# The mix of two branches: loops written out, the result kept on chip, the output weights loaded into the normed rows' place

## The chip, the cores and the metric

One NeuronCore of one Trainium2 chip runs the whole program: a first block (attention with compressed keys beside an RWKV branch, a gated mix, a mixture of experts) and two further layers (windowed attention and a recurrent layer, each with experts). The metric is the device time of one execution in microseconds. TensorE does the matrix products, VectorE and ScalarE the elementwise work, SyncE issues most of the DMA transfers. Everything is in float32, and each float32 product of 128 x 128 by 128 x 512 shows as two matmul records.

## The reference, cut to what matters

```python
gates = sigmoid(z_gate + gate_b)                  # (T, 2, D); z_gate = h @ w_in[:, gate columns]
# o_rwkv: y = y_f + y_b, normed over each head of 64:
mu = mean(y); var = mean(square(y - mu))
y = (y - mu) * rsqrt(var + LNX_EPS) * lnx_g + lnx_b
o_rwkv = (y + bonus) * g
mixed = gates[:, 0] * (o_mla @ w_br_mla) + gates[:, 1] * (o_rwkv @ w_br_rwkv)
x = x + mixed @ w_out
h2 = rms_norm(x, norm_ffn_g)                      # then router logits, top 2 of 32 experts
```

T = 1024 tokens, D = 1024 channels; `o_mla` and `o_rwkv` have 512 channels each.

## The kernel before, in words

Each stage is a `Phase`: it owns its on-chip tensors and semaphores and ends with a clearing of the semaphores and a barrier of all engines (line 83 is the barrier). Within a phase each engine has its own program, and semaphores order them. There is no planner; the order on each engine is the order of the code.

**`mix_phase`** holds data transposed: 128 channels on the partitions, 1024 tokens along the row. `h_h_all` (the normed input, `hT` in the code) is on chip already. It has two loops.

The gate loop (4 turns, `j`) computes four gates per turn, gate `2j+u` of branch `b`: 8 products by K and 2 halves of the tokens (`many`, line 1371) into PSUM `pb[2+b]`, and a sigmoid on ScalarE (line 1411) into `sg`, which has room for all 16 gates. Beside them runs the head norm of row block `j` of the RWKV branch: VectorE adds the two directions (`y`, line 1433), TensorE sums over heads with the `ones` matrix (`two`, line 1365), VectorE subtracts the mean (1435), ScalarE squares (1418), TensorE sums again, VectorE makes the variance (1437), ScalarE takes the root (1421), and VectorE inverts it, scales, adds the bonus and multiplies by `g` into `oT` (1439 to 1443); `o_ready` then counts. The sum over `y` stands between gates `(0,0)` and `(0,1)`, the sum over the squares between `(0,1)` and `(1,0)`.

SyncE loads per turn the weights of both branches' gates for `u` = 0 and 1 (line 1336, two places of `wg`, each reused when `z_psum` says that its products are done), then, once `o_ready` says that the one place of `inp` is free, the two y rows (1340), bonus and g (1341, 1342). VectorE waits for all four. `vecs` and `head_ones` are the first two loads of the phase (1329, 1330), and all engines wait for both.

The branch loop (4 turns of 2 blocks) computes `oT` by `w_br_mla` and by `w_br_rwkv`, 16 products per block into two PSUM tensors (line 1371 again). VectorE multiplies both by their gates (1454), adds them (1456) into one of two places `mixed`, and SyncE stores it to `mixT` in DRAM (1351, 1353). `wb` has two places, loaded at line 1348. In SyncE's order the store of a block, with its wait for `mixed_ready`, stands ahead of the weights of the next turn. The phase ends when SyncE has seen all stores land.

**`route_phase`** is written out. SyncE loads the first 256 tokens of `mixT` (line 1579), then half of `w_out`, one x tile, the other half, another x tile (1581, 1582), seven constants (1588) and the rest of `mixT` (1589). TensorE multiplies token tile by token tile, in halves of the columns (`product`, line 1624), with the turning of h2 (1635) and the router's logits (1643) of the tile before in between. VectorE adds x (1696), norms, and at the end works out the choice of experts and the order of the rows.

**`experts_phase`** loops over blocks of 128 gathered rows, with expert weights in two places for pairs of blocks: `wb[0]` belongs to `Moe`, `wb[1]` (`wb1`) and `w2b[1]` to the phase, as do the turned rows `xT`.

At the top, phase "h" (which owns `h_h_all`) ends behind `mix_phase`; `Moe` opens behind it.

Of the kernel before, what the change touches and what calls it, by code (L numbers as in the profile page):

```python
# [13 lines left out]
P = 128  # L14
# [1275 lines left out]
def mix_phase(nc, vecs, w_in, w_br_mla, w_br_rwkv, head_ones, hT, oT_dram, arr_dram, y_dram, mixT_dram):  # L1290

    with Phase(nc, "mix") as ph:
        vec = ph.sb("vec", [P, VEC_N])
# [12 lines left out]
        names = "in_done y_sum mean_psum cent sq_ready var_psum root o_ready consts o_in rt_ready z_psum gates br_psum mixed_ready mixed_out".split()  # L1307
        (in_done, y_sum, mean_psum, cent, sq_ready, var_psum, root, o_ready, consts, o_in, rt_ready, z_psum, gates, br_psum, mixed_ready,
         mixed_out) = [ph.sem(n) for n in names]
        wg_done = [ph.sem(f"wg_done{u}") for u in range(2)]  # L1310
        wb_done = [ph.sem(f"wb_done{u}") for u in range(2)]
        V, A, E, S = (ph.engine(e, n) for e, n in ((nc.vector, "dve"), (nc.scalar, "act"), (nc.tensor, "pe"), (nc.sync, "sp")))
# [3 lines left out]
        mix_view = mixT_dram.rearrange("(k p) t -> p k t", p=P)  # L1316
        wi = w_in[0].rearrange("(k p) n -> p k n", p=P)
        wa = w_br_mla[0].rearrange("(k p) n -> p k n", p=P)
        wr = w_br_rwkv[0].rearrange("(k p) n -> p k n", p=P)

        with nc.Block() as block:

            @block.sync
            def _(sp):
                S.open(in_done, n=64)
                S.open(mixed_out, n=32)
                for u in range(2):
                    S.open(wg_done[u], wb_done[u], n=32)
                sp.dma_start(vec[:, :], vecs).then_inc(consts, 16)
                sp.dma_start(ones[:, :], head_ones).then_inc(consts, 16)  # L1330
                with sp.Fori(0, RJ) as j:
                    for u in range(2):

                        S.hold(z_psum, last(j, 4, 2 * u + 2))
                        for b in range(2):
                            sp.dma_start(wg[:, u, b, :, :], wi[:, :, ds(j * (2 * P) + (GATE_AT + b * D + u * P), P)]).then_inc(wg_done[u], 16)

                    S.hold(o_ready, last(j))
                    for n in range(2):
                        sp.dma_start(inp[:, n:n + 1, :], y_view[:, n, ds(j, 1), :]).then_inc(in_done, 16)  # L1340
                    sp.dma_start(inp[:, 2:3, :], arr_view[:, ARR["bonus"], ds(j, 1), :]).then_inc(in_done, 16)
                    sp.dma_start(inp[:, 3:4, :], arr_view[:, ARR["g"], ds(j, 1), :]).then_inc(in_done, 16)
                sp.dma_start(oT[:, 0:RJ, :], oT_dram.rearrange("(k p) t -> p k t", p=P)).then_inc(o_in, 16)
                with sp.Fori(0, KD // 2) as i:
                    for u in range(2):
# [11 lines left out]
            def _(pe):  # L1357
# [17 lines left out]
                with pe.Fori(0, RJ) as j:  # L1375

                    def gate(u, b):
                        if b == 0:
                            E.hold(wg_done[u], now(j, 32))
# [2093 lines left out]
```

## Time and profile before

| | us |
|---|---|
| three runs, median (lowest, highest) | 4792.51 (4784.24, 4794.08) |
| the profiled execution | 4792.43 |
| its span, first to last instruction | 4790.5 |
| TensorE busy | 4221.4 (88%) |
| VectorE busy | 1579.2 (33%) |
| ScalarE busy | 1072.3 (22%) |
| mean granted TensorE clock | 0.945 of full |
| mix phase, first product to the routing's first product | 1165.44 to 1574.16 |

A row of the timeline merges the instructions of one line that follow each other: its start in us from the start of the span, its length, the engine, the line, what is written from what, how many; in brackets how long the engine stood idle ahead of it and what ended that. PE is TensorE, DVE is VectorE, ACT is ScalarE, SPq is the issuing of DMAs by SyncE. Ends of matmuls are modelled, so a distance is read from start to start.

### The profile page before, as it was taken

The numbers are of one execution on the slowest core, as the hardware profiler recorded it, in microseconds if no ns is written. First come the engines' busy times: TensorE is split into PE (matmuls) and PEld (weight loads), VectorE is DVE, ScalarE is ACT, GpSimd is POOL, SyncE is SP. The second block draws the span as 40 slices with busy tenths as digits, with TensorE's granted clock in tenths as the row PEclk, the third lists the DMA queues.
The fourth block names the chain that finished last, engine by engine and source line by source line (L and its number), as shares of the span: only waits on it lengthen the run. The fifth ranks groups of instructions, "written<-read, shape, count | busy, mean of one in ns | idle before, by whom it ended". The sixth has DMA issues, their size and how long they took to land. (4 is left out here: it accounts for less than half of the span.)

```text
span 4790.5 us, 62335 instructions
## 1 busy us (share of the span) xinstructions
PE 4221.4 (88%) x23090; PEld 2185.5 (46%) x23091; DVE 1579.2 (33%) x2933; ACT 1072.3 (22%) x1830; POOL 267.3 (6%) x304
## 2 busy tenths in 40 slices
PE   7899996887997879988899599999799995999995
PEld 4555444775443444434454344444344442444442
DVE  3365364442221132213483611011156445011012
ACT  1155122443110001111263100000146331000002
POOL 0000001221000001010000000000000000000000
PEclk8899998999998989999999799999899997999998
DMA  2040244332211469964103388888521143888884
GB/s 92 30 172 10 61 171 119 86 79 61 74 63 52 165 217 371 357 232 163 49 1 128 138 302 314 311 310 311 189 68 40 53 160 146 310 304 315 310 310 165
DMA packets 419890, 815.46 MB, mean 170 GB/s; under 512 B 140784, under 2 KB 281968, under 8 KB 386800
## 3 DMA queue, kind: packets, MB, share of 16 engines
q1 hardware_dynamic: 390912, 711.35, 42.9%
q0 software_dynamic: 16704, 60.82, 4.4%
q10 hardware_dynamic: 12080, 40.54, 2.1%
q8 instruction: 142, 2.33, 0.2%
q14 instruction: 52, 0.43, 0.0%
HBM read 686.80 MB, written 125.83 MB: 170 GB/s over the span
## 5 line engine op out<-in xcount | busy, mean ns | idle before, releaser
L2848 PE MATMUL ec0e_pg<-ec_wg,ec0e_xT 128*128 128x512 f32 x1024 | 444.8, 595 | 2.2 <-DVE ec0e_xT L2901 2.2
L2848 PE MATMUL ec1e_pg<-ec_wg,ec1e_xT 128*128 128x512 f32 x1024 | 444.4, 594 | 2.1 <-DVE ec1e_xT L2901 2.1
L2848 PEld LDWEIGHTS ec0e_pg<-ec_wg,ec0e_xT 128*128 128x128 f32 x1024 | 195.4, 191 | 248.7 <-issue 248.7
L2848 PEld LDWEIGHTS ec1e_pg<-ec_wg,ec1e_xT 128*128 128x128 f32 x1024 | 195.3, 191 | 248.3 <-issue 248.3
L1371 PE MATMUL mix_pb<-h_h_all,mix_wg 128*128 128x512 f32 x512 | 224.0, 598 | 12.1 <-DMA mix_wg<-in_w_in_dram 12.1
L3132 PE MATMUL lrui_pA<-lrui_xT,lrui_w 128*128 128x512 f32 x512 | 223.8, 597 | 2.6 <-ACT lrui_xT L3206 2.6
L2874 PE MATMUL ec1e_py<-lru_wd,ec1e_hidT 128*128 128x512 f32 x512 | 223.4, 594 | 0.0
L2874 PE MATMUL ec0e_py<-gqa_wd,ec0e_hidT 128*128 128x512 f32 x512 | 223.3, 594 | 0.0
L679 PE MATMUL front_pz<-h_h_all,front_w 128*128 128x512 f32 x480 | 211.5, 598 | 9.0 <-DMA front_ones<-in_head_ones_dram 9.0
L2889 ACT ACTIVATE ec1e_sg<-ec1e_pg 128x512 f32<-128x512 f32 x32 | 19.2, 599 | 650.0 <-PE ec1e_pg L2848 650.0
L2889 ACT ACTIVATE ec0e_sg<-ec0e_pg 128x512 f32<-128x512 f32 x32 | 19.2, 599 | 648.5 <-PE ec0e_pg L2848 648.5
L2909 DVE TENSOR_TENSOR ec0e_hid<-ec0e_sg,ec0e_pg 128x512 f32<-128x512 f32 x32 | 22.0, 689 | 426.9 <-ACT ec0e_sg L2889 426.9
L2909 DVE TENSOR_TENSOR ec1e_hid<-ec1e_sg,ec1e_pg 128x512 f32<-128x512 f32 x32 | 22.0, 689 | 426.4 <-ACT ec1e_sg L2889 426.4
L1371 PEld LDWEIGHTS mix_pb<-h_h_all,mix_wg 128*128 128x128 f32 x512 | 98.2, 192 | 135.8 <-issue 135.8
L3132 PEld LDWEIGHTS lrui_pA<-lrui_xT,lrui_w 128*128 128x128 f32 x512 | 97.8, 192 | 125.6 <-issue 125.6
L972 POOL TENSOR_TENSOR wkv_a_l<-wkv_a_raw,wkv_tab 128x512 f32<-128x512 f32 x80 | 106.4, 1363 | 786.1 <-ACT wkv_a_raw L988 786.1
L679 PEld LDWEIGHTS front_pz<-h_h_all,front_w 128*128 128x128 f32 x480 | 91.2, 192 | 127.2 <-issue 127.2
L2874 PEld LDWEIGHTS ec1e_py<-lru_wd,ec1e_hidT 128*128 128x128 f32 x512 | 96.0, 190 | 115.5 <-issue 114.8
L2874 PEld LDWEIGHTS ec0e_py<-gqa_wd,ec0e_hidT 128*128 128x128 f32 x512 | 96.0, 190 | 115.3 <-issue 114.8
L1371 PE MATMUL mix_pb<-mix_oT,mix_wb 128*128 128x512 f32 x256 | 119.1, 629 | 32.9 <-DMA mix_wb<-in_w_br_rwkv_dram 30.9
L459 PE MATMUL mlaa_pS<-mla_kT,mla_qT 96*128 96x512 f32 x256 | 129.7, 631 | 4.6 <-ACT mlaa_probs L522 2.5
L1624 PE MATMUL route_po<-route_wo,route_mT 128*128 128x512 f32 x256 | 114.4, 601 | 20.3 <-DMA route_wo<-in_w_out_dram 20.3
(550 smaller groups left out, 6259.4 us busy)
## 6 DMA issues: line engine op xcount, KB each, us to landing
ec_wg<-in_moe_w_gate_up_dram SPq DMA_DIRECT2D x256, 1024.0 KB, 6.5
gqa_wd<-in_moe_w_down_dram SPq DMA_DIRECT2D x128, 512.0 KB, 4.4
lru_wd<-in_moe_w_down_dram SPq DMA_DIRECT2D x128, 512.0 KB, 4.4
moe_wb<-in_w_dram SPq DMA_DIRECT2D x32, 1024.0 KB, 12.7
exp_wb<-in_w_dram SPq DMA_DIRECT2D x32, 1024.0 KB, 12.6
wkv_inp<-arrays SPq DMA_DIRECT2D x160, 128.0 KB, 3.0
arrays<-front_out SPq DMA_DIRECT2D x36, 512.0 KB, 5.7
yb<-mlaa_zero SPq DMA_DIRECT2D x1, 16384.0 KB, 50.6
```

Of the source, the lines that this page charges most:

```text
L459: m = nc.tensor.matmul(pS[:, u % 2 * 2 + j, :], q_all[:, head, tile * P:(tile + 1) * P], k_all[:, head, j * HALF:(j + 1) * HALF], start=Tr ...
L679: m = nc.tensor.matmul(pz[q % 2][:, half * HALF:(half + 1) * HALF], w[:, q % U, k, :], hT[:, k, half * HALF:(half + 1) * HALF], start=k == ...
L972: nc.gpsimd.tensor_tensor(grid(a_l[:, n, :]), grid(a_raw[:, :]), mask(n + 1), ALU.mult).then_inc(a_masked, 1)
L1371: m = nc.tensor.matmul(ps[:, half * HALF:(half + 1) * HALF], weights[:, k, :], rhs[:, k, half * HALF:(half + 1) * HALF], start=k == 0, sto ...
L1624: m = nc.tensor.matmul(po[:, t % 2, halves[h]], mT[:, k, t * P:(t + 1) * P], wo[:, k, halves[h]], start=k == 0, stop=k == KD - 1)
L2848: return nc.tensor.matmul(pg[:, b, :], xT[:, k, :], wg[:, k, b * HALF:(b + 1) * HALF], start=k == 0, stop=k == KD - 1)
L2874: m = nc.tensor.matmul(py[:, b * HALF:(b + 1) * HALF], hidT[:, k, :], wd[:, k, b * HALF:(b + 1) * HALF], start=k == 0, stop=k == KD - 1)
L2889: nc.scalar.activation(sg[:, half * HALF:(half + 1) * HALF], pg[:, half, :], ACT.Silu).then_inc(silu, 1)
L2909: nc.vector.tensor_tensor(hid[:, cols], sg[:, cols], pg[:, 2 + half, :], ALU.mult).then_inc(hid_ready, 1)
L3132: m = nc.tensor.matmul(pA[:, bank, :], w[:, q % W_RING, k, :], xT[:, k, halves[h]], start=k == 0, stop=k == KD - 1)
```

## The change

In `mix_phase` every loop is written out. The weights of a gate have three places (`RING`) and are loaded gate by gate; the two small constants are loaded from ScalarE's queue; the y rows and the bonus and g rows have semaphores of their own. Only gates 0 to 3 (both branches) are computed beside the head norm: two per row block instead of four. Gates 4 to 7 alternate with branch blocks 0 to 3, and `sg` keeps four blocks' gates instead of eight. The branch weights have three places too, and from block 4 on the blocks alternate between two pairs of PSUM tensors. VectorE writes the mixed rows to `mixT`, which is now an on-chip tensor; nothing is stored to DRAM. When the last gate's products are done, SyncE loads the first half of `w_out` into the columns of `hT`, and after the last branch weights the second half. `route_phase` takes both from there and loads neither. `experts_phase` uses `h_h_all` and `mixT` as its second weight buffers and for `xT`. The phase that owns `h_h_all` and a new one that owns `mixT` end behind the experts.

```diff
-def mix_phase(nc, vecs, w_in, w_br_mla, w_br_rwkv, head_ones, hT, oT_dram, arr_dram, y_dram, mixT_dram):
+def mix_phase(nc, vecs, w_in, w_br_mla, w_br_rwkv, head_ones, hT, oT_dram, arr_dram, y_dram, mixT, w_out, wo_in):
...
+        RING, SLOT = 3, 4
...
-        wg = ph.sb("wg", [P, 2, 2, KD, P])
-        wb = ph.sb("wb", [P, 2, 2, RJ, P])
-        sg = ph.sb("sg", [P, 2, KD, T])
-        mixed = ph.sb("mixed", [P, 2, T])
+        wg = ph.sb("wg", [P, RING, KD, P])
+        wb = ph.sb("wb", [P, RING, 2, RJ, P])
+        sg = ph.sb("sg", [P, SLOT, 2, T])
...
+            return (pb[2], pb[3]) if i >= 4 and i % 2 else (pb[0], pb[1])
...
+                def load_g(q):
+                    i, b = q // 2, q % 2
+                    if q >= RING:
+                        sp.wait_ge(z_psum, q - RING + 1)
+                    sp.dma_start(wg[:, q % RING, :, :], wi[:, :, GATE_AT + b * D + i * P:GATE_AT + b * D + (i + 1) * P]).then_inc(wg_in[q % RING], 16)
+                def load_b(i):
+                    if i >= RING:
+                        sp.wait_ge(br_psum, i - RING + 1)
+                    for b, src in enumerate((w_br_mla, w_br_rwkv)):
+                        sp.dma_start(wb[:, i % RING, b, :, :], src[0, :, i * P:(i + 1) * P].rearrange("(k p) n -> p k n", p=P)).then_inc(wb_in[i % RING], 16)
+                def load_y(j):
+                    if j:
+                        sp.wait_ge(o_ready, j)
                     for n in range(2):
-                        sp.dma_start(inp[:, n:n + 1, :], y_view[:, n, ds(j, 1), :]).then_inc(in_done, 16)
-                    sp.dma_start(inp[:, 2:3, :], arr_view[:, ARR["bonus"], ds(j, 1), :]).then_inc(in_done, 16)
-                    sp.dma_start(inp[:, 3:4, :], arr_view[:, ARR["g"], ds(j, 1), :]).then_inc(in_done, 16)
+                        sp.dma_start(inp[:, n:n + 1, :], y_view[:, n, j:j + 1, :]).then_inc(y_in, 16)
+                def load_bonus(j):
+                    sp.dma_start(inp[:, 2:3, :], arr_view[:, ARR["bonus"], j:j + 1, :]).then_inc(bonus_in, 16)
+                    sp.dma_start(inp[:, 3:4, :], arr_view[:, ARR["g"], j:j + 1, :]).then_inc(bonus_in, 16)
+                load_g(0)
+                load_y(0)
+                load_g(1)
+                load_bonus(0)
+                load_g(2)
                 sp.dma_start(oT[:, 0:RJ, :], oT_dram.rearrange("(k p) t -> p k t", p=P)).then_inc(o_in, 16)
-                with sp.Fori(0, KD // 2) as i:
-                    for u in range(2):
-                        S.hold(br_psum, last(i, 2, u + 1))
-                        for b, src in enumerate((wa, wr)):
-                            sp.dma_start(wb[:, u, b, :, :], src[:, :, ds(i * (2 * P) + u * P, P)]).then_inc(wb_done[u], 16)
-                        if u:
-                            S.hold(mixed_ready, now(i, 2, u))
-                            sp.dma_start(mix_view[:, ds(i * 2, 1), :], mixed[:, 0:1, :]).then_inc(mixed_out, 16)
-                    S.hold(mixed_ready, now(i, 2, 2))
-                    sp.dma_start(mix_view[:, ds(i * 2 + 1, 1), :], mixed[:, 1:2, :]).then_inc(mixed_out, 16)
-                sp.wait_ge(mixed_out, 16 * (KD + 2))
+                for i in range(RING):
+                    load_b(i)
+                for j in range(1, RJ):
+                    load_g(2 * j + 1)
+                    load_y(j)
+                    load_bonus(j)
+                    load_g(2 * j + 2)
+                load_g(9)
...
+                load_g(10)
+                for i in range(3, 6):
+                    load_b(i)
+                    load_g(2 * i + 5)
+                    if i < 5:
+                        load_g(2 * i + 6)
+                load_b(6)
+                sp.wait_ge(z_psum, 2 * KD)
+                sp.dma_start(hT[:, :, halves[0]], w_out[0, :, halves[0]].rearrange("(k p) n -> p k n", p=P)).then_inc(wo_in[0], 16)
+                load_b(7)
+                sp.dma_start(hT[:, :, halves[1]], w_out[0, :, halves[1]].rearrange("(k p) n -> p k n", p=P)).then_inc(wo_in[1], 16)
...
+                def gate(i, b, h):
+                    q = 2 * i + b
+                    if h == 0:
+                        pe.wait_ge(wg_in[q % RING], 16 * (q // RING + 1))
+                        if i:
+                            pe.wait_ge(gates, q - 1)
+                    for k in range(KD):
+                        m = nc.tensor.matmul(pb[2 + b][:, halves[h]], wg[:, q % RING, k, :], hT[:, k, halves[h]], start=k == 0, stop=k == KD - 1)
+                    if h == 1:
+                        m.then_inc(z_psum, 1)
...
+                def branches(i):
+                    pe.wait_ge(wb_in[i % RING], 32 * (i // RING + 1))
+                    if i == 0:
+                        pe.wait_ge(o_in, 16)
+                        pe.wait_ge(o_ready, RJ)
+                    elif i == 5:
+                        pe.wait_ge(gates, 2 * KD)
+                        pe.wait_ge(products, 4)
+                    else:
+                        pe.wait_ge(products, i if i < 5 else i - 1)
...
+                for j in range(RJ):
+                    gate(j, 0, 0)
+                    pe.wait_ge(y_sum, j + 1)
+                    if j == 0:
+                        pe.wait_ge(ones_in, 16)
+                    sums(pb[0], y).then_inc(mean_psum, 1)
+                    gate(j, 0, 1)
+                    pe.wait_ge(sq_ready, j + 1)
+                    sums(pb[1], sq).then_inc(var_psum, 1)
+                    gate(j, 1, 0)
+                    gate(j, 1, 1)
+                for i in range(RJ):
+                    branches(i)
+                    for b in range(2):
+                        gate(RJ + i, b, 0)
+                        gate(RJ + i, b, 1)
+                for i in range(RJ, KD):
...
+                    branches(i)
...
+                act.dma_start(ones[:, :], head_ones).then_inc(ones_in, 16)
+                act.dma_start(vec[:, :], vecs).then_inc(v_in, 16)
+                act.wait_ge(v_in, 16)
+                def gate(i, b):
+                    act.wait_ge(z_psum, 2 * i + b + 1)
+                    if i >= SLOT:
+                        act.wait_ge(products, i - SLOT + 1)
...
+                    dve.wait_ge(y_in, 32 * (j + 1))
+                    if j == 0:
+                        dve.wait_ge(v_in, 16)
...
+                def mixed(i):
+                    dve.wait_ge(br_psum, i + 1)
+                    dve.wait_ge(gates, 2 * i + 2)
+                    for b, dst in enumerate((mixT[:, i, :], m1[:, :])):
+                        r = nc.vector.tensor_tensor(dst, banks(i)[b][:, :], sg[:, i % SLOT, b, :], ALU.mult)
+                    r.then_inc(products, 1)
+                    dve.wait_ge(products, i + 1)
+                    V.link(nc.vector.tensor_tensor(mixT[:, i, :], mixT[:, i, :], m1[:, :], ALU.add))
...
-def route_phase(nc, x, w_out, rg_w, rg_b, re_w, re_b, vecs, eye, tables, mixT_dram, x1_dram, h2_dram, slot_u, wts, moe):
+def route_phase(nc, x, wo, wo_in, mT, rg_w, rg_b, re_w, re_b, vecs, eye, tables, x1_dram, h2_dram, slot_u, wts, moe):
...
-        wo = ph.sb("wo", [P, KD, D])
...
-        mT = ph.sb("mT", [P, KD, T])
...
-                sp.dma_start(mT[:, :, 0:EARLY], mix_view[:, :, 0:EARLY]).then_inc(early, 16)
                 for h in range(2):
-                    sp.dma_start(wo[:, :, halves[h]], w_out[0, :, halves[h]].rearrange("(k p) n -> p k n", p=P)).then_inc(wo_in[h], 16)
...
-                sp.dma_start(mT[:, :, EARLY:T], mix_view[:, :, EARLY:T]).then_inc(late, 16)
...
-                pe.wait_ge(early, 16)
...
-                        pe.wait_ge(late, 16)
...
-        wb = [moe.wb[0], ph.sb("wb1", [P, 2, 2, KD, D_EXP])]
-        w2b = [moe.w2b[0], ph.sb("w2b1", [P, 2, 2, D])]
+        wb = [moe.wb[0], spare[0][:, :, :].rearrange("p (u n k) t -> p u n (k t)", u=2, n=2).rearrange("p u n (k f) -> p u n k f", k=KD)]
+        w2b = [moe.w2b[0], spare[1][:, 0:4, :].rearrange("p (u k) d -> p u k d", u=2)]
...
-        xT = ph.sb("xT", [P, R, KD, P])
+        xT = spare[1][:, 4:8, :].rearrange("p s (k t) -> p s k t", k=KD)
...
+        with Phase(nc, "h") as shared:
+            h_all = shared.sb("h_all", [P, KD, T])
+            h_in = shared.sem("h_in")
+            mla_phase(nc, I["x"], I["vecs"], I["w_in"], I["w_uq"], I["w_ukv"], I["eye"], I["mla_rope"], hT, oT, h_all, h_in, yb)
+            front_phase(nc, I["vecs"], I["w_in"], h_all, h_in, I["w_up"], I["a_up"], I["g_up"], I["starts"], I["head_ones"], arrays)
+            wkv_phase(nc, I["wkv_tables"], I["eye"], arrays, yT)
+            with Phase(nc, "mixed") as second:
+                mixT = second.sb("mixT", [P, KD, T])
+                wo_in = [second.sem(f"wo_in{h}") for h in range(2)]
+                mix_phase(nc, I["vecs"], I["w_in"], I["w_br_mla"], I["w_br_rwkv"], I["head_ones"], h_all, oT, arrays, yT, mixT, I["w_out"], wo_in)
+                with Phase(nc, "moe") as third:
+                    moe = Moe(third, I["w1"], I["w3"], I["w2"])
+                    route_phase(nc, I["x"], h_all, wo_in, mixT, I["router_group_w"], I["router_group_b"], I["router_expert_w"],
+                                I["router_expert_b"], I["vecs"], I["eye"], I["route_tables"], x1, h2, slots, weights, moe)
+                    experts_phase(nc, moe, (h_all, mixT), h2, yb)
```

## Rows read from the trace of the kernel before

**Rows 1.** Page, part 1: busy us, share of the span, instructions.

```profile
PE 4221.4 (88%) x23090; PEld 2185.5 (46%) x23091; DVE 1579.2 (33%) x2933; ACT 1072.3 (22%) x1830; POOL 267.3 (6%) x304
```

**Rows 2.** Page, part 5: busy, mean ns, idle before and its releaser.

```profile
L1371 PE MATMUL mix_pb<-h_h_all,mix_wg 128*128 128x512 f32 x512 | 224.0, 598 | 12.1 <-DMA mix_wg<-in_w_in_dram 12.1
...
L1371 PE MATMUL mix_pb<-mix_oT,mix_wb 128*128 128x512 f32 x256 | 119.1, 629 | 32.9 <-DMA mix_wb<-in_w_br_rwkv_dram 30.9
...
L1624 PE MATMUL route_po<-route_wo,route_mT 128*128 128x512 f32 x256 | 114.4, 601 | 20.3 <-DMA route_wo<-in_w_out_dram 20.3
```

**Rows 3.** Timeline, TensorE, gate loop: start us, us, what, idle before.

```profile
1165.44 16.65 PE L1371 MATMUL mix_pb<-h_h_all,mix_wg 128*128 128x512 f32 x32 [12.09 <-DMA mix_wg<-in_w_in_dram]
...
1181.93 1.88 PE L1365 MATMUL mix_pb<-mix_y,mix_ones 128*128 128x512 f32 x4
...
1183.65 13.90 PE L1371 MATMUL mix_pb<-h_h_all,mix_wg 128*128 128x512 f32 x32
...
1197.38 1.88 PE L1365 MATMUL mix_pb<-mix_sq,mix_ones 128*128 128x512 f32 x4
```

**Rows 4.** Timeline, SyncE's queue, start of the mix phase.

```profile
1158.00 0.35 SPq L1329 DMA_DIRECT2D mix_vec<-in_vecs_dram  x1
...
1159.26 3.72 SPq L1336 DMA_DIRECT2D mix_wg<-in_w_in_dram  x4
```

**Rows 5.** DMA issues: KB, us to landing; first line gate weights, last line `w_out`.

```profile
DMA to landing us min/median/max: 4.0/5.1/7.0
...
mix_inp<-yT SPq DMA_DIRECT2D x2, 512.0 KB, 6.0
...
mixT<-mix_mixed SPq DMA_DIRECT2D x2, 512.0 KB, 2.7
...
route_xt<-in_x_dram SPq DMA_DIRECT2D x4, 512.0 KB, 4.0
...
DMA to landing us min/median/max: 11.2/13.6/16.0
```

**Rows 6.** Timeline, TensorE, two groups of branch products.

```profile
1403.84 27.70 PE L1371 MATMUL mix_pb<-mix_oT,mix_wb 128*128 128x512 f32 x64 [2.01 <-issue]
...
1442.05 30.32 PE L1371 MATMUL mix_pb<-mix_oT,mix_wb 128*128 128x512 f32 x64 [10.51 <-DMA mix_wb<-in_w_br_rwkv_dram]
```

**Rows 7.** Windows: us, busy by engine, granted clock, DMA share, GB/s.

```profile
1442.00:1447.00 5.00, 4.95 (x6) 2.19 (x7) 0.00 (x0) 0.00 (x0) 0.00 (x0) 0.50 0.05 15
...
2750.00:2950.00 200.00, 196.41 (x516) 91.16 (x515) 21.05 (x24) 15.79 (x25) 11.16 (x12) 1.00 0.87 307
...
1840.00:1940.00 100.00, 98.98 (x295) 48.18 (x294) 23.33 (x35) 13.87 (x22) 10.38 (x18) 1.00 1.04 363
```

**Rows 8.** Timeline, VectorE, first and last of a normed row's chain.

```profile
1199.41 1.23 DVE L1437 TENSOR_SCALAR mix_rt<-mix_pb 128x1024 f32<-128x1024 f32 x1 [14.22 <-PE mix_pb L1365]
...
1213.94 1.23 DVE L1443 TENSOR_TENSOR mix_oT<-mix_y,mix_inp 128x1024 f32 x1 [0.26 <-DVE mix_y L1442]
```

**Rows 9.** Timeline, all engines, from the mix phase to the routing.

```profile
1556.78 1.22 DVE L1456 TENSOR_TENSOR mix_mixed<-mix_mixed,mix_m 128x1024 f32<-128x1024 f32 x1
1558.39 0.37 SPq L1353 DMA_DIRECT2D mixT<-mix_mixed  x1
...
1574.16 22.26 PE L1624 MATMUL route_po<-route_wo,route_mT 128*128 128x512 f32 x48 [20.32 <-DMA route_wo<-in_w_out_dram]
```

**Rows 10.** Timeline, TensorE, two short stands in later phases.

```profile
2179.24 7.13 PE L2164 MATMUL gqap_pq<-gqa_wd,gqap_xT 128*128 128x512 f32 x16 [3.08 <-DMA gqa_wd<-in_attn_w_qkv_dram]
...
3711.06 10.16 PE L3161 MATMUL lrui_pB<-lru_wd,lrui_gw 128*128 128x512 f32 x16 [3.24 <-ACT lrui_buf L3220]
```

**Rows 11.** Timeline, all engines, change from attention to its tail.

```profile
2539.66 0.42 DVE L2445 TENSOR_TENSOR gqa_oT<-gqaa_ou,gqaa_pO 128x256 f32<-128x256 f32 x1 [2.45 <-ACT gqaa_ou L2397]
...
2540.91 1.52 PE L2566 MATMUL ec0p_po<-gqa_wd,gqa_oT 128*128 128x512 f32 x3 [1.70 <-PEq L83]
```

**Rows 12.** Timeline, TensorE, written-out products of the routing.

```profile
1602.27 10.55 PE L1624 MATMUL route_po<-route_wo,route_mT 128*128 128x512 f32 x24
```

More of the change, by code:

```diff
@@ L1375, in _ @@
[L1375 to L1379, printed above, removed]
-                        E.hold(gates, now(j, 4, 2 * u + b - 1) if u else last(j, 4, 3 + b))
-                        many(pb[2 + b], wg[:, u, b, :, :], KD, hT).then_inc(z_psum, 1)
-                    gate(0, 0)
-                    E.hold(y_sum, now(j))
-                    two(pb[0], ones[:, :], y).then_inc(mean_psum, 1)
-                    gate(0, 1)
-                    E.hold(sq_ready, now(j))
-                    two(pb[1], ones[:, :], sq).then_inc(var_psum, 1)
-                    gate(1, 0)
-                    gate(1, 1)
@@ L1392, in _ @@
-                E.hold(o_ready, RJ + 1)
-                E.hold(gates, 4 * (RJ + 1))
-                pe.wait_ge(o_in, 16)
-                with pe.Fori(0, KD // 2) as i:
-                    for u in range(2):
-                        E.hold(wb_done[u], now(i, 32))
-                        E.hold(mixed_ready, last(i, 2, u + 1))
-                        many(pb[2 * u], wb[:, u, 0, :, :], RJ, oT)
-                        many(pb[2 * u + 1], wb[:, u, 1, :, :], RJ, oT[:, RJ:2 * RJ, :]).then_inc(br_psum, 1)
+                def gate(i, b, h):
[8 more added lines that the diff above has]
+                        m.then_inc(z_psum, 1)
@@ L1442, in _ @@
                     V.link(nc.vector.tensor_tensor(y[:, :], y[:, :], inp[:, 2, :], ALU.add))
-                    V.link(nc.vector.tensor_tensor(oT[:, ds(j + RJ, 1), :].rearrange("p o t -> p (o t)"), y[:, :], inp[:, 3, :], ALU.mult))
+                    V.link(nc.vector.tensor_tensor(oT[:, RJ + j, :], y[:, :], inp[:, 3, :], ALU.mult))
                     dve.sem_inc(o_ready, 1)
-                V.done(RJ)
-                dve.wait_ge(gates, 4 * (RJ + 1))
-                with dve.Fori(0, KD // 2) as i:
-                    V.loop(i, 4)
-                    for u in range(2):
-                        V.hold(br_psum, now(i, 2, u + 1))
-                        V.hold(mixed_out, last(i, 32, 16 * (u + 1)))
-                        for b, dst in enumerate((mixed[:, u, :], m1[:, :])):
-                            r = nc.vector.tensor_tensor(dst, pb[2 * u + b][:, :], sg[:, b, ds(i * 2 + u, 1), :].rearrange("p o t -> p (o t)"), ALU.mult)
-                        V.link(r)
-                        V.link(nc.vector.tensor_tensor(mixed[:, u, :], mixed[:, u, :], m1[:, :], ALU.add))
-                        dve.sem_inc(mixed_ready, 1)
@@ L1461 @@
+                for j in range(RJ):
+                    normed(j)
+                for i in range(KD):
+                    mixed(i)
 N_GROUPS, PER_GROUP = 4, 8
@@ L1563, in route_phase @@
          first_e, in_ready, pos_ready, i_psum, idx_ready) = [ph.sem(n) for n in names]
-        early, late = ph.sem("early"), ph.sem("late")
-        wo_in = [ph.sem(f"wo_in{h}") for h in range(2)]
         x_in = [ph.sem(f"x_in{u}") for u in range(2)]
```

118 lines of the change are left out of this document (38 added, 80 removed).

## The prediction

> **What bounds the kernel now.** I read the granted clock of the one core first, then the page, then its costliest groups, TensorE's waits, the stretches of the mix phase, and last the timelines of each engine in that phase and at its two edges. TensorE is busy 88% of the span [rows 1], so a change counts by the time for which TensorE stands still or runs at half clock. In the stage that is edited, the 512 gate products stand still once (12.1 us) and the 256 branch products 32.9 us (30.9 of them for `mix_wb`), and the routing's products 20.3 us for `route_wo` [rows 2]. Those are what the change can take; the matmuls themselves stay. VectorE's share of the span says nothing here. Its long chain per normed row (part 3) hides behind four gates now, and the change takes away half of that cover.
>
> **Yardsticks.** The product of one gate (32 recorded matmuls) starts at 1183.65 and the next group at 1197.38, so it is 13.73 us; the sum over heads (4 matmuls) is 1.72 us (1181.93 to 1183.65) [rows 3]. All 16 gates, 8 pairs of branch products and 8 sums are computed before and after, in the same instructions: 24 x 13.73 + 8 x 1.72 = 343.3 us of TensorE, unchanged. The sum is made against the profiled execution, 4792.43 us (span 4790.5 us and 1.9 us around it), which is the median of the three runs (4792.51) for all purposes.
>
> **Part 1, the start (+2.9).** TensorE starts at 1165.44 [rows 3]. SyncE's first issue is at 1158.00, but two small loads go first, the weights are issued from 1159.26 on in four issues of 0.93 us each, and TensorE waits for both gates' weights [rows 4]. After, the two small loads go on ScalarE's queue, the gate's weights are the first issue and TensorE waits for those alone. A 512 KB load of gate weights lands 4.0 to 7.0 us after issue (median 5.1) [rows 5]; on an empty queue I take 4.5, so the start is 1162.5, 2.9 us earlier (0.4 to 3.4). The y rows come second (1 MB); their add is wanted after half a gate, 9.6 us after the start with the cold clock, and they have that.
>
> **Part 2, the branch stalls (+39.2).** Now SyncE waits for `mixed_ready` ahead of the next weights, so each second pair of blocks starts late, as at 1442.05 after 10.51 us [rows 6]; there are three of these, 30.9 us [rows 2]. All four groups are busy 119.1 us [rows 2] where 4 x 27.70 = 110.8 would do: 8.3 us. After, weights have three places and are asked for one to three blocks ahead: the nearest case, `load_b(3)`, goes out when the first branch block is done and is wanted after two more blocks and six gates. A load twice its size takes 5.1 us [rows 5]. The wait on `products` ahead of a branch block is covered too: VectorE needs two products and TensorE has two gates (27 us) in between, and from block 5 on the PSUM pairs alternate. 30.9 + 8.3 = 39.2 us go.
>
> **Part 3, what is late next: the y rows (-5.1).** The gate loop now has two gates per normed row, not four, and `load_y(j+1)` still waits for `o_ready`, since there is one `inp`. Count from the start v of the sum of squares (1197.38 [rows 3]). VectorE reads it at 1199.41, and its last product starts at 1213.94 and takes 1.23, so `o_ready` is at v + 17.8 [rows 8]. Then 0.4 us to SyncE's issue (the add ends at 1558.0, the store is issued at 1558.39 [rows 9]), 0.45 for the second issue, the landing, and 1.23 for the add with 0.2 of hand-over. For the landing the nearest row is a 512 KB load right behind another transfer of that size: 4.0 us (`route_xt`); the y rows' own median of 6.0 has two gates' weights ahead of it, which will not be there [rows 5]. y is ready at v + 24.1. TensorE wants it at v + 1.72 + 13.73 + 6.87 = v + 22.3. So it stands 1.7 us, in each of three loops (the first rows are there in time): 5.1 us. Bounds per loop: 0.4 us with the landing of an isolated store (2.7 [rows 5]) and 3.7 us with 6.0, and on top the clock, next.
>
> What a short stand costs in clock, rows show as well: 2.01 us ahead of the branch products cost nothing (27.70 us for 64 is 0.43 each [rows 6]); behind 3.08 us, 16 matmuls took 7.13 us, and behind 3.24 us 10.16 [rows 10], where by the 13.90 for 32 [rows 3] 7.0 would do: 0.1 and 3.1 us. So 1.7 us is taken at nothing. Ends for the three loops together: 1.2 and 3 x (3.7 + 3.1) = 20.4 us.
>
> The Trainium skill speaks against this edit: "TensorE: Matmul & The Clock Gate", section "HAM oscillation — how this bites in real kernels", says that a loop whose products are interrupted by a wait for a DMA each time pays the slow clock again on every turn. By that rule with the price of the worst row, the three loops would cost some 14 us and not 5.1; the trace agrees with it for the wait of 3.24 us and shows no cost at 2.01. It is the first rival below, whose time is worked out without it.
>
> **Part 4, gates to branches (-0.4).** The first branch block now waits for the fourth normed row: `o_ready` at v + 17.8, 0.1 of hand-over, TensorE done at v + 15.5: 2.4 us, where it stood 2.01 before [rows 6]. From here on TensorE has 8 branch blocks and 8 gates, 220 us, with no wait that I can find: a gate's PSUM is free when the sigmoid of two gates earlier is done, and each sigmoid waits for `products` of a block that was finished a gate ago.
>
> **Part 5, the edge to the routing (+13.9).** Now VectorE ends at 1558.0, the store goes out at 1558.39, SyncE waits for it and the barriers and issues the routing's loads, and TensorE starts at 1574.16, when half of `w_out` is there [rows 9]. After, there is no store, the mixed rows are on chip, and `w_out` is asked for when the last gate is done: 55 us of branch products are left, 41 us for its second half, against 11.2 to 16.0 us for such a load now (median 13.6 [rows 5]). What is left is the barrier: in another phase change VectorE ends at 2540.08 and TensorE starts at 2540.91, 0.83 us later [rows 11]. I take 1.0, so the start is 15.2 us earlier (14.4 to 15.4). The routing starts at half clock before and after: it costs 1.5 us now (22.26 for 48 matmuls [rows 9] where 20.8 would do), and I take the 2.8 of the mix phase's own start (16.49 for 13.73 [rows 3]), so -1.3 (+1.5 to -1.3). The x rows and constants are issued at once; they now land behind 4 MB of weights and will then have the queue alone. The first use of the constants is 22 us after TensorE's start.
>
> **Part 6, the rest (-0.5).** Of the barriers at phase ends, one goes from this edge and two are added behind the experts; with the last instructions around it one takes 0.83 us at most [rows 11], and I take 0.5 (0 to 0.8). The experts' second buffers lie in the places of the normed and the mixed rows, but are filled by the same loads at the same points. The written-out products cost nothing: the routing is written out already, and there 24 matmuls take 10.55 us [rows 12], and by the loop's 13.90 for 32 they would take 10.5.
>
> **The sum:** 2.9 + 39.2 - 5.1 - 0.4 + 13.9 - 0.5 = 50.0 us. 4792.4 - 50.0 = 4742.4 us. All of it stays, since everything behind hangs on the routing's result and only starts sooner.
>
> **Rivals.**
> (a) The y rows come late enough for the clock to fall: 6.0 us of landing, so 3 x 3.7 = 11.1 us, and the mean of the two priced stands (0.1 and 3.1) on each, 4.8: 15.9 for 5.1, 4753 us; at worst 20.4, 4758. For it: the 6.0 row, and that the bonus and g rows are issued right behind. Against: `route_xt`'s 4.0.
> (b) The output weights don't do what they are fetched early for: some transfer still holds the routing's start for 10 us. 4752 us. Against: 41 us of cover.
> (c) The gain is swallowed by the experts, whose loads run at 363 GB/s [rows 7]: 4790 us, no change. Against: TensorE is busy 99.0 of 100 us there, and the loads need the routing's choice, so they move with it.
> (d) Slower: straight-line code. The loops' bodies are replaced by 800 matmuls in a row with their weight loads; if these had to be fetched at a pace below TensorE's, each would need to start 62 ns later (0.492 for 0.430 us) to eat the 50 us, and at 0.50 the kernel takes 4799 us. Against it stands the routing's row [rows 12].
> (e) The longer unbroken run (220 us) is granted a lower clock: against it, 200 us of the later experts at clock 1.00 [rows 7]; it counts with (d).
>
> **Chances.** Forecast 78%, (a) 13%, (b) 3%, (c) 3%, (d) and (e) together 3%. A measurement of this kernel can tell 0.2%, 9.6 us, from no change. Faster: 0.94; same 0.03; slower 0.03. Low end: 1.2 for the loops, no loss at the edge's clock, 0.5 at the start, 4736.7, and single runs lie up to 8 us apart around the median: 4733. High end: rival (a) with 4 us more, 4757.
>
> **What will show it.** Right: TensorE starts near 1162.5; three waits of 1 to 3 us for VectorE's y in the gate loop, followed by groups without loss; one of 2.4 us ahead of the first branch block; then no wait and clock 1.00 until the last product, near 1516.6; the routing's first product 5.3 us behind it. Wrong: waits of over 3 us for y with half clock behind them (a); a DMA as releaser of the routing's first product (b); the stretch behind the routing longer than before (c); a mean distance of matmuls above 0.43 us at clock 1.00 (d).

## The result, and the profile after

| us | before | after |
|---|---|---|
| median of the runs (lowest, highest) | 4788.47 (4784.24, 4794.08), 4 runs | 4734.23 (4731.53, 4735.47), 4 runs |
| profiled execution, its span | 4792.43, 4790.5 | 4735.36, 4733.2 |
| mean granted clock | 0.945 | 0.949 |

The ratio is 0.9882, 95% interval 0.9868 to 0.9897: 1.2% faster. The medians are 54.2 us apart, the profiled executions 57.1; the forecast was 50.0. (The prediction's sum starts at the profiled execution of the kernel before, 4792.43 us, which lies 4.0 us above the median of the four runs.) Taken again later, beside new runs of the kernel before, the changed kernel took 4732.67 us (4725.16 to 4733.73, 5 runs), 0.9878 of it (0.9862 to 0.9895).

The page's groups of the changed kernel that answer to [rows 2], with the idle time behind the last bar:

```profile
L1385 PE MATMUL mix_pb<-h_h_all,mix_wg 128*128 128x512 f32 x512 | 224.6, 598 | 8.8 <-DMA mix_wg<-in_w_in_dram 8.8
...
L1646 PE MATMUL route_po<-h_h_all,mixed_mixT 128*128 128x512 f32 x256 | 115.5, 606 | 5.2 <-PEq L83 5.2
```

The branch products are no longer in the list: they don't wait for weights any more. TensorE's timeline through the mix phase into the routing (start, length, what, how many; in brackets a stand ahead and what ended it):

```profile
1162.16 9.73 PE L1385 MATMUL mix_pb<-h_h_all,mix_wg 128*128 128x512 f32 x16 [8.81 <-DMA mix_wg<-in_w_in_dram]
1171.73 1.88 PE L1391 MATMUL mix_pb<-mix_y,mix_ones 128*128 128x512 f32 x4
...
1180.31 1.88 PE L1391 MATMUL mix_pb<-mix_sq,mix_ones 128*128 128x512 f32 x4
1182.03 20.76 PE L1385 MATMUL mix_pb<-h_h_all,mix_wg 128*128 128x512 f32 x48
1202.63 1.88 PE L1391 MATMUL mix_pb<-mix_y,mix_ones 128*128 128x512 f32 x4
...
1274.73 13.90 PE L1385 MATMUL mix_pb<-h_h_all,mix_wg 128*128 128x512 f32 x32
1288.66 11.82 PE L1407 MATMUL mix_pb<-mix_oT,mix_wb 128*128 128x512 f32 x27
...
1453.54 55.10 PE L1407 MATMUL mix_pb<-mix_oT,mix_wb 128*128 128x512 f32 x128
1513.87 23.38 PE L1646 MATMUL route_po<-h_h_all,mixed_mixT 128*128 128x512 f32 x48 [5.24 <-PEq L83]
```

No bracket stands between the first gate and the routing: the y rows are never late, and the first branch block starts 0.2 us behind the last gate (1288.66 against 1274.73 + 13.73). From 1302 to 1450 the clock is full:

```profile
1162.16:1168.00 5.84, 5.84 (x8) 2.51 (x9) 1.23 (x1) 0.00 (x0) 0.00 (x0) 0.55 1.07 397
1302.00:1450.00 148.00, 148.00 (x346) 65.55 (x345) 14.32 (x12) 7.79 (x7) 0.00 (x0) 1.00 0.12 32
```

(Window, its length, busy time by engine, granted clock, DMA share, GB/s.) From 1162.16 to 1168.00 it is 0.55, near the lower of the two levels. The gain of the span, 57.3 us, is this:

| | before | after | gain | forecast |
|---|---|---|---|---|
| end of the stage before (1153.35 in both) to the first gate product | 12.09 | 8.81 | 3.3 | 2.9 |
| first gate product to the last branch product | 388.4 | 346.5 | 41.9 | 33.7 |
| last branch product to the routing's first | 20.3 | 5.2 | 15.1 | 15.2 |
| from there to the end of the span | 3216.3 | 3219.3 | -3.0 | -1.8 |

### The profile page after: what moved, and what is told of

Read it like the earlier page. It is cut to its first block and busy times, and to the rows that moved or that the text cites. A ratio compares the mean times of both kernels' runs of the same rounds, so it can differ in the third digit from the quotient of the medians.

```text
span 4733.2 us, 61819 instructions
## 1 busy us (share of the span) xinstructions
PE 4216.9 (89%) x23090; PEld 2186.2 (46%) x23091; DVE 1578.3 (33%) x2933; ACT 1068.2 (23%) x1827; POOL 267.2 (6%) x304
## 5 line engine op out<-in xcount | busy, mean ns | idle before, releaser
L3180 PE MATMUL lrui_pB<-lru_wd,lrui_gw 128*128 128x512 f32 x256 | 117.8, 619 | 6.5 <-ACT lrui_buf L3239 6.5
L1646 PE MATMUL route_po<-h_h_all,mixed_mixT 128*128 128x512 f32 x256 | 115.5, 606 | 5.2 <-PEq L83 5.2
```

The costliest lines, as they stand in the source:

```text
L1646: m = nc.tensor.matmul(po[:, t % 2, halves[h]], mT[:, k, t * P:(t + 1) * P], wo[:, k, halves[h]], start=k == 0, stop=k == KD - 1)
L3180: m = nc.tensor.matmul(pB[:, at, :], gw[:, u % 2, z, k, c, :], xc[:, u // 2 * 2 + c, halves[h]], start=c == 0, stop=c == 1)
```

## The experiments

**1. Why the normed rows are not late.** The changed kernel's ScalarE and VectorE in the first turn:

```profile
1180.51 1.11 ACT L1440 ACTIVATE mix_sg<-mix_pb,mix_vec 128x1024 f32<-128x1024 f32 x1 [3.19 <-PE mix_pb L1385]
1181.64 1.28 ACT L1449 ACT_TABLE_LOAD   x1
1183.49 1.06 ACT L1449 ACTIVATE mix_rt<-mix_rt 128x1024 f32<-128x1024 f32 x1 [0.56 <-DVE mix_rt L1466]
```
```profile
1182.23 1.22 DVE L1466 TENSOR_SCALAR mix_rt<-mix_pb 128x1024 f32<-128x1024 f32 x1 [7.36 <-PE mix_pb L1391]
1184.58 6.55 DVE L1470 RECIPROCAL mix_rt<-mix_rt 128x1024 f32<-128x1024 f32 x1 [1.12 <-ACT mix_rt L1449]
...
1194.53 1.23 DVE L1474 TENSOR_TENSOR mix_oT<-mix_y,mix_inp 128x1024 f32<-128x1024 f32 x1
1200.83 1.23 DVE L1462 TENSOR_TENSOR mix_y<-mix_inp 128x1024 f32<-128x1024 f32 x1 [5.07 <-DMA mix_inp<-yT]
```

The table of the square root is loaded at 1181.64, before `rt` exists (VectorE is done with it at 1183.45); ScalarE then waits. In the kernel before, the load came behind that wait, since VectorE's `rt` ended the gap ahead of it:

```profile
1200.74 1.28 ACT L1421 ACT_TABLE_LOAD   x1 [1.84 <-DVE mix_rt L1437]
```

From the start v of the sum of squares, v = 1180.31, `o_ready` is at v + 15.45, where it was at v + 17.8 [rows 3, 8]. Theory A: that is the form of the wait. In the loops each wait was an instruction of its own with a semaphore increment behind it (`hold`); written out, it is a plain wait against a constant. Rival B is that the chain got shorter by something else, fewer loads beside it or constant addresses. Two runs put the increment back:

```diff
                     act.wait_ge(rt_ready, j + 1)
+                    act.sem_inc(A.pace, 1)
                     nc.scalar.activation(rt[:, :], rt[:, :], ACT.Sqrt).then_inc(root, 1)
```

> The changed kernel with one semaphore increment between ScalarE's wait for rt_ready and the square root, so that the wait stands alone, as it does in the loops of the kernel before. Theory A (in the written-out program the load of ScalarE's table goes ahead of the wait, and that is most of why the chain of a normed row is shorter than forecast): the table load moves behind rt again, VectorE's reciprocal starts about 3.6 us behind the start of rt and not 2.35, the chain grows by 1.3 us, the y rows come 0.7 us late in each of three turns and the first branch block by 1.3 us; the mix phase takes about 3.4 us longer. Rival B (the chain is shorter because the loads beside it are fewer or the addresses constant): nothing moves.

```profile
1181.27 1.28 ACT L1451 ACT_TABLE_LOAD   x1 [1.94 <-DVE mix_rt L1468]
1182.56 1.06 ACT L1451 ACTIVATE mix_rt<-mix_rt 128x1024 f32<-128x1024 f32 x1
```
```profile
1201.37 1.98 PE L1392 MATMUL mix_pb<-mix_y,mix_ones 128*128 128x512 f32 x4 [0.87 <-DVE mix_y L1464]
...
1290.83 13.97 PE L1408 MATMUL mix_pb<-mix_oT,mix_wb 128*128 128x512 f32 x32 [1.40 <-DVEq L1477]
```

The table load is behind `rt` again, `o_ready` is at v + 16.8 (15.45 in the changed kernel), and TensorE stands 0.87, 0.66 and 0.76 us for y and 1.40 ahead of the branches: 3.7 us where it stood 0.2, as expected (3.4 us more). (The one time taken, 4731.33 us, can't show 3.5 us: single runs of one kernel lie up to 17 us apart, and a good part of that is spent ahead of this stage, whose predecessor ended anywhere between 1149.0 and 1158.1 us in the profiles.) The second run adds, to that increment, `dve.sem_inc(V.pace, 1)` behind the wait ahead of the reciprocal and behind each of VectorE's five chained steps:

> The same increment on ScalarE and one behind the wait ahead of the reciprocal and behind each of the five chained steps of VectorE, as the loops of the kernel before have them. Theory A with its second half (each such stand-alone wait costs VectorE some 0.15 us): the chain from the start of the second sum to o_ready is 17.8 us again as before (15.45 in the changed kernel), TensorE stands 1.7 us for the y rows in three turns and 2.4 us ahead of the first branch block, and the kernel takes some 7 us longer, close to the forecast 4742. Rival B: no more than 1 us longer.

```profile
1201.30 1.98 PE L1392 MATMUL mix_pb<-mix_y,mix_ones 128*128 128x512 f32 x4 [1.42 <-DVE mix_y L1464]
...
1292.68 15.67 PE L1408 MATMUL mix_pb<-mix_oT,mix_wb 128*128 128x512 f32 x32 [2.09 <-DVEq L1483]
```

```profile
1177.40 1.88 PE L1392 MATMUL mix_pb<-mix_sq,mix_ones 128*128 128x512 f32 x4
```
```profile
1193.59 1.22 DVE L1481 TENSOR_TENSOR mix_oT<-mix_y,mix_inp 128x1024 f32<-128x1024 f32 x1
```

`o_ready` is at v + 17.4, and TensorE stands 1.42, 1.35, 1.31 and 2.09 us (1.7, three times, and 2.4 expected), with 1.7 us of half clock behind the last (15.67 for 13.97), which was not expected. From the first gate product to the last branch product it takes 8.5 us more than the changed kernel. The time is 4741.66 us (4738.49 to 4745.15, 4 runs; 0.9905 of before, 0.9888 to 0.9921). That is 0.7 us from the forecast, but in part by luck, since the half clock makes up for stands that were shorter than forecast; and its interval overlaps that of the changed kernel (0.9868 to 0.9897), so the trace shows the difference and the time only suggests it.

Theory A holds for most of the chain: of the 2.35 us, the place of the table load is 1.36 and the increments on VectorE are 0.6. The last 0.4 us didn't come back, and what they were is not shown; rival B may have a share in them. So the forecast priced a chain with the old form of waits.

**2. What a stand costs in clock, rival (a).** Three runs let the y rows come later, by asking ahead of them for loads that stand behind them in the changed kernel (and, in the third, for a row that nothing reads):

```diff
 # 1 MB ahead                  # 1.5 MB ahead                # 2 MB ahead
+sp.wait_ge(o_ready, j)       +sp.wait_ge(o_ready, j)       +sp.wait_ge(o_ready, j)
+load_bonus(j)                +load_bonus(j)                +load_bonus(j)
                              +load_g(2 * j + 2)            +load_g(2 * j + 2)
                                                            +sp.dma_start(extra, y_view[:, 0, 0:1, :]) ...
 load_y(j)                     load_y(j)                     load_y(j)
```

> The changed kernel with the bonus and g rows (1 MB) asked for ahead of the y rows. The y rows should land 2.8 us later (1 MB at some 370 GB/s), so TensorE stands about 2.2 us in each of three turns. Theory C (a stand this short costs no clock): the group of 16 matmuls behind it stays at 7.03 us, the kernel takes 6.6 us longer. Rival D, rival (a) of the forecast (a stand repeated in every turn drops the clock): groups of 8 to 10 us behind each, 10 to 15 us longer in all.

> As the run with the bonus rows first, with the next gate weights (512 KB) ahead of the y rows as well: 1.5 MB, so a stand of about 3.6 us in each of three turns. If the price in clock sets in at about 3 us, as the two rows of the kernel before say (0.1 us behind 3.08, 3.1 behind 3.24), the matmuls behind each cost between 0 and 3 us more; if short stands never cost clock, nothing: 11 us longer in all without the clock, up to 20 with it.

> As the run with the bonus rows first, and the next gate weights and one more load of 512 KB (a y row again, into a place that nothing reads) ahead of the y rows too: 2 MB, so the y rows land some 5.6 us later and TensorE stands about 5 us in each of three turns. Theory C (the price in clock grows with the length of the stand): each costs 1.5 to 3.1 us in the matmuls behind it, 20 to 24 us longer in all. Rival: stands alone, 15 us longer, the groups behind them unchanged.

TensorE in the second turn of each, in this order of the kernels:

```profile
1201.09 3.38 PE L1392 MATMUL mix_pb<-mix_y,mix_ones 128*128 128x512 f32 x4 [2.66 <-DVE mix_y L1463]
1204.31 7.03 PE L1386 MATMUL mix_pb<-h_h_all,mix_wg 128*128 128x512 f32 x16
```
```profile
1201.67 3.78 PE L1392 MATMUL mix_pb<-mix_y,mix_ones 128*128 128x512 f32 x4 [3.26 <-DVE mix_y L1463]
1205.25 8.17 PE L1386 MATMUL mix_pb<-h_h_all,mix_wg 128*128 128x512 f32 x16
```
```profile
1208.82 3.78 PE L1398 MATMUL mix_pb<-mix_y,mix_ones 128*128 128x512 f32 x4 [4.52 <-DVE mix_y L1469]
1212.39 7.45 PE L1392 MATMUL mix_pb<-h_h_all,mix_wg 128*128 128x512 f32 x16
```

The sum of four matmuls takes 1.98 behind a short stand and 3.78 at half clock, the 16 gate matmuls 7.03 at full clock. With the two runs of experiment 1, that makes 17 stands:

| stand, us | how many | lost in the matmuls behind it |
|---|---|---|
| 0.66 to 1.42 | 7 | nothing |
| 2.01, 2.09, 2.58, 2.66 | 4 | 0, 1.7, 0, 1.4 |
| 3.26 to 5.28 | 6 | 1.8 to 3.0 each |

The first gate product to the last four blocks took 300.8, 312.1 and 311.5 us against 291.4 in the changed kernel: 9.4, 20.7 and 20.2 longer, for 6.6, 11 to 20 and 20 to 24 expected; the times were 4740.66, 4750.44 and 4756.71 us, one run each. The stands were 2.4, 4.0 and 4.5 us on average (2.2, 3.6 and 5 expected). So rival (a) had a real price, but its condition, late y rows, didn't come about in the changed kernel. No stand of the forecast's 1.7 us was measured: the nearest are 1.42 (free), 2.01 (free, here and in [rows 6]) and 2.09 (1.7 us lost). From 2.0 to 2.7 us some stands lose the clock; all of 3.26 us and over did. The kernel before has one of 3.08 us that cost 0.1 [rows 10].

**3. The branch stalls alone.** The kernel before, with SyncE's part of the branch loop written out and in another order, and nothing else (the store semaphore is split in two for it). There SyncE asked for the weights only behind the store, 5 us before TensorE's product at 1442.05:

```profile
1436.10 0.37 SPq L1353 DMA_DIRECT2D mixT<-mix_mixed  x1
1437.06 0.41 SPq L1348 DMA_DIRECT2D mix_wb<-in_w_br_mla_dram  x1
```

The new order:

```diff
+                for n in range(KD):
+                    if n + 2 < KD:
+                        sp.wait_ge(br_psum, n + 3)
+                        load_b(n + 2)
+                    sp.wait_ge(mixed_ready, n + 3)
+                    sp.dma_start(mix_view[:, n:n + 1, :], ...)
```

> The kernel before with one part alone: SyncE asks for a branch block's weights as soon as the products of two blocks earlier are done, ahead of the store of mixed rows, in its two places; everything else, the loops too, stays. Theory (the stalls are SyncE's order, not the number of places): the three waits of 10 us and the half clock behind them go, 39 us faster. Rival (two places are too few, or the store and the loads disturb each other): waits of some us stay, under 30 us faster.

```profile
1408.50 110.11 PE L1377 MATMUL mix_pb<-mix_oT,mix_wb 128*128 128x512 f32 x256 [2.01 <-issue]
```

All eight blocks in one run of 110.11 us, in two places of weights. 4753.80 us (4748.08 to 4759.62, 4 runs), 0.9919 of before (0.9903 to 0.9936): 31 to 46 us. In the trace the stage is 388.4 - 348.3 = 40.1 us shorter, 39 expected. Most of the change's gain is this order on one queue; a third place, the unrolled loops of the other engines and the interleaving are not needed for it.

**4. The edge.** Two runs of the changed kernel undo it step by step: first the two loads of `w_out` go back to the start of the routing, then the mixed rows also go to DRAM block by block, the phase waits for the stores, and the routing loads them again.

```diff
-                sp.dma_start(hT[:, :, halves[0]], w_out[0, :, halves[0]]...
+                for h in range(2):          # in the routing
+                    sp.dma_start(wo[:, :, halves[h]], w_out[0, :, halves[h]]...
```

> The changed kernel with the output weights loaded in the routing again, as before, into the same place. Theory: the mixed rows on chip bring little by themselves, since the weights still have to land: TensorE starts the routing some 8 us later than in the changed kernel (its two loads landed in 7.4 us median there), 8 to 10 us longer. Rival (the barrier and the reload of the mixed rows were the wait, the weights came beside them): under 3 us longer.

> As the run before this one, and the mixed rows are stored to DRAM and loaded again in the routing, as before: the edge as the kernel before has it. The last block's store and its landing cost about 3 us ahead of the barrier, and 1 MB of mixed rows ahead of the weights another 3: 14 to 15 us longer than the changed kernel. If it costs less, part of the edge's gain has another source than these two edits.

```profile
1519.96 22.73 PE L1644 MATMUL route_po<-h_h_all,mixed_mixT 128*128 128x512 f32 x48 [12.76 <-DMA h_h_all<-in_w_out_dram]
```
```profile
1526.60 22.57 PE L1655 MATMUL route_po<-h_h_all,mixed_mixT 128*128 128x512 f32 x48 [17.52 <-DMA h_h_all<-in_w_out_dram]
```

Stands of 12.8 and 17.5 us for 5.2: 7.5 us for the weights (8 to 10 expected), 4.8 more for the way through DRAM, 12.3 together (14 to 15 expected). The times are 4740.91 (4739.07 to 4741.65) and 4743.45 us (4739.47 to 4746.52), four runs each (0.9897 and 0.9900 of before); their intervals, 0.9880 to 0.9913 and 0.9883 to 0.9916, overlap each other's and the changed kernel's, so these prices are read in the trace. The kernel before stood 20.3, so 2.8 of the 15.1 us belong to neither: 1.3 lie between the last product and the first load (one phase end more, and the looped tail), 1.5 in a slower landing of the first half (11.7 against 10.2 us from SyncE's first issue to the product). That rest wasn't separated further.

**5. Keeping TensorE busy across the two waits.** Three products that nothing reads while the first weights are on their way, and some behind the last block:

```diff
+                for n in range(3):
+                    nc.tensor.matmul(pb[1][:, 0:HALF], hT[:, 0, 0:P], hT[:, 0, 0:HALF], start=True, stop=True)
...
+                for n in range(5):
+                    nc.tensor.matmul(pb[0][:, 0:HALF], ones[:, :], oT[:, 0, 0:HALF], start=True, stop=True)
```

> The changed kernel with eight products more, whose results nothing reads: three at the start of the mix phase, while the first gate's weights are on their way, and five behind the last branch block, while VectorE finishes the mixed rows. Theory C (half clock is the price of the stand ahead of it, and work of any kind avoids it): the first 16 gate matmuls take some 7.5 us and not 9.7, the routing's first 48 take 20.8 and not 23.4, so some 4.5 us shorter in the trace, a tenth of a per cent. Rival: the clock falls at the phase change anyway (the barrier's 1 us), then the routing's 23 us stay.

> As the run kept warm, and the last branch block computed by halves of the tokens, so that VectorE multiplies and adds the first half while TensorE computes the second. VectorE's tail ahead of the barrier shrinks from 4.5 us to some 2.5: 2 us on top of the run kept warm, 6 to 7 us under the changed kernel. If the tail is not what the barrier waits for, nothing on top.

> As the run by halves, with three products that nothing reads behind the last block and not five. In the run by halves VectorE ended 2.6 us behind the last real product but TensorE's filler only after 4.45, and the routing began 5.3 us behind that product, as without halves. If the filler held the barrier, the routing now begins 3.5 us behind the last product and its first 48 matmuls still take 20.8 us: 1.8 us shorter in the trace from the last product on. Rival: the barrier costs the 5.3 us whatever ends ahead of it, or the clock falls in the gap and the 48 take over 22 us.

> The changed kernel once more, on the chip of the two others, to compare with: 4728 to 4740 us.

The run by halves, and then the one with the shorter filler, from the filler to the routing:

```profile
1507.50 4.45 PE L1439 MATMUL mix_pb<-mix_oT,mix_ones 128*128 128x512 f32 x10
1512.82 20.84 PE L1666 MATMUL route_po<-h_h_all,mixed_mixT 128*128 128x512 f32 x48 [0.86 <-PEq L83]
```
```profile
1507.12 2.74 PE L1439 MATMUL mix_pb<-mix_oT,mix_ones 128*128 128x512 f32 x6
1510.86 20.84 PE L1666 MATMUL route_po<-h_h_all,mixed_mixT 128*128 128x512 f32 x48 [1.00 <-PEq L83]
```

The clock holds over the 1 us of the barrier: 20.84 us for 48 matmuls, for 23.38. In the run kept warm the first 16 gate matmuls take 7.39 for 9.73 (8.86 to 10.14 in the runs without filler). But three products at half clock last 5.5 us, longer than the wait that they fill: the first gate product came 9.6 us behind the stage before and not 8.8, so the start gained 1.6 us. Halves alone brought nothing (5.3 us from the last product to the routing, as before), because the filler had become what the barrier waits for; with the shorter one it is 3.7. From the end of the stage before to the end of the routing's first 48, the changed kernel takes 383.7 us (383.1 the second time), kept warm 379.6, by halves 379.6, with the shorter filler 377.1. The times are 4727.02 (0.9868, 0.9850 to 0.9887), 4732.52 (0.9877, 0.9861 to 0.9894) and 4728.30 us (0.9867, 0.9850 to 0.9883) beside 4732.67 (0.9878) for the changed kernel: the intervals of the ratios overlap, so the 6.6 us are seen in the trace and not in the time.

## Why the prediction was right or wrong

The direction, the places and their order were right, and 4734.23 us lies in the range, but 1.2 us above its low end, and in the profiled executions the gain was 7 us larger than the sum. Those 7 us are the 5.1 of part 3 and the 2.2 of part 4; the smaller errors of the other parts cancel.

- **Part 3 failed (-5.1 forecast, 0 measured)**, and with it **part 4 (-0.4 forecast, +1.8)**. The step was "`o_ready` is at v + 17.8": it took VectorE's chain from the loop of the kernel before. Measured v + 15.45. What follows in that step came out: y was wanted at v + 22.3 (22.32: the sum of squares at 1180.31, the next sum over y at 1202.63), and from the chain's end to the add it took 5.07 us where its terms give 5.05. The second is partly luck: SyncE issued 0.1 us behind `o_ready` and not 0.4, and landing and hand-over took 4.6 us and not 4.2. y was there at v + 21.75, 0.6 us ahead. Experiment 1 gives 2.0 of the 2.35 us back, and the stands come with them. The omission stands in part 6: "the written-out products cost nothing" looked at TensorE alone and never asked what unrolling does to ScalarE and VectorE.
- **Part 2 (39.2)** was right in its mechanism and 0.9 us short (40.1 in experiment 3): 27.70 for an undisturbed group holds 0.2 us of modelled end, which was counted into each of four groups, and 0.2 us of the 40.1 are a shorter half clock at that run's first gate.
- **Part 1** 3.3 for 2.9: SyncE's first issue was at 1157.64, 0.4 us earlier, and the weights landed in the assumed 4.5.
- **Part 5**: the start 15.1 us earlier for 15.2, and half clock behind it (23.38, 2.6 us lost, for 2.8). The mechanism was right, the closeness is luck twice. From the end of VectorE's last add (1511.12 + 1.23 = 1512.35, the line below) the barrier took 1.5 us and not 1.0, but VectorE ended 3.7 us behind the last product and not 4.2 as in the kernel before; and the first 48 matmuls took 22.42 to 23.74 us in seven profiles with the changed kernel's edge, and 23.41 in experiment 3 with the old edge (22.26 in the kernel before's one profile), so the clock's -1.1 us need not come from the change. Experiment 4 says which edit brings what: the early weights 7.5 us, the rows kept on chip 4.8.

```profile
1511.12 1.23 DVE L1484 TENSOR_TENSOR mixed_mixT<-mixed_mixT,mix_m 128x1024 f32<-128x1024 f32 x1
```

- **Part 6 (-0.5)**: all that lies behind the routing's first product came to -3.0 with the clock's -1.1 in it. Two stands grew, at the start of the experts and behind them (before, then after):

```profile
1750.24 1.94 PE L1900 MATMUL exp_pt<-moe_ident,moe_xg 128*128 128x128 f32 x8 [10.29 <-PEq L83]
2163.90 1.94 PE L2150 MATMUL gqap_pt<-gqa_ident,gqap_x 128*128 128x128 f32 x8 [31.16 <-DVE gqap_x L2237]
```
```profile
1692.98 1.94 PE L1919 MATMUL exp_pt<-moe_ident,moe_xg 128*128 128x128 f32 x8 [11.35 <-PEq L83]
2107.43 1.94 PE L2169 MATMUL gqap_pt<-gqa_ident,gqap_x 128*128 128x128 f32 x8 [32.41 <-DVE gqap_x L2256]
```

  Every profile has them: 10.3 and 31.1 to 31.2 us in the two that leave the experts as they were (experiment 3's is the other), 11.1 to 11.9 and 32.2 to 32.6 in the twelve of the changed kernel and its variants. Behind the experts the program has two phase ends more, so the 1.2 us there is most likely these. The forecast took 0.5 (at most 0.8), because it set the barrier that goes from the routing's edge against them, which part 5's start had counted already. Why the experts start 1 us later is open.
- **Rivals.** (a) did not come, since there was no stand at all; its price is now measured. (b) to (e) did not come: 5.2 us at the edge (b), 378.4 us from the experts' first product to the start of their last, where it was 378.8 (c), and 0.43 us per matmul in 346 recorded, written-out ones at clock 1.00 (d, e). The prediction's "near 1516.6" for the last product doesn't follow from its own terms, which give 1517.1; it ended at 1508.6.

## What to carry to other kernels

Look first for a queue that waits for a result ahead of a load that doesn't need it: that alone was 40 of the 57 us here, and half clock behind each wait was a fifth of it. When loops become straight-line code, recount every engine's chain, not only the busiest one's: here the waits' form was worth 2.0 us of a chain per turn and decided whether TensorE stood. In these runs a stand of up to 1.4 us cost only its own length, one of 3.3 to 5.3 us 1.8 to 3.0 us more. Filler must not outlast what it fills: ahead of a barrier it has to end no later than the engine that the barrier waits for, and ahead of a load no later than the load.

## What the runs showed of the hardware

- ScalarE's table load runs ahead of a plain wait (1181.64, with `rt` ready at 1183.45) and behind a wait that an increment follows (1181.27 in experiment 1, [1.94 <-DVE]): `o_ready` comes 1.36 us later in each turn.
- The length of a stand does not decide alone on the clock: 2.58 us cost nothing and 2.09 cost 1.7.
- Full clock outlasts a barrier if products run up to it: behind a gap of 1.00 us the next 48 matmuls take 20.84 us, behind one of 5.24 us 23.38.
- An increment behind each wait of VectorE's chain costs it 0.6 us (v + 17.4 in the second run of experiment 1, v + 16.8 in the first), with five of them ahead of the last product.
